# Seven products in a four-sum form, extended to the mixers' input projection, in a macaron block kernel

## What is computed

```python
def swiglu_ffn(h, w_in, w_out):                    # w_in (2048, 2*5632), w_out (5632, 2048)
    gate, up = jnp.split(h @ w_in, 2, axis=-1)
    return (jax.nn.silu(gate) * up) @ w_out

def mixer_block(h, w_in, b_in, ...):
    z = h @ w_in + b_in                            # 2048 -> 1024 pool | 2048 conv | 4096 gates
    pooled = causal_multiscale_pool(u_pool)        # windows 2, 4, 8, 16
    a  = (group_map(pooled) * pool_scale) @ pool_w_proj
    c  = causal_depthwise_conv(glu(u_conv))        # 31 taps
    bb = silu(layernorm(c)) @ conv_w_proj
    return (sigmoid(g_a) * a + sigmoid(g_b) * bb) @ w_out

x = x + 0.5 * swiglu_ffn(rmsnorm(x), ffn1...)
x = x + mixer_block(rmsnorm(x), ...)
x = x + 0.5 * swiglu_ffn(rmsnorm(x), ffn2...)
return rmsnorm(x)
```

## Time and profile before

| | before |
|---|---|
| median of 3 runs | 4974.64 us |
| profiled execution, slowest core (6) | 4988.0 us |
| other cores in it | 4966.1 to 4980.6 us |
| TensorE busy | 4608.7 us (92%), 24754 matmuls |
| VectorE busy | 3335.2 us (67%) |
| ScalarE busy | 1409.4 us (28%) |
| DMA from GpSimd's queue | 407.40 MB, 52.8% of the 16 engines' span |
| DMA from SyncE's queue | 330.97 MB, 20.7% |
| mean granted TensorE clock | 0.972 of 2.4 GHz |

### The profile page before, as it was taken

One profiled execution on the slowest core, in us unless ns is written; L12 is line 12 of the kernel. 1 busy time (PEld: TensorE's weight loads), 2 busy tenths in 40 slices (PEclk: granted clock), 3 DMA queues, 4 the chain that ended last, 5 costly groups with the idle time before them and its releaser, 6 DMA issues.

```text
span 4988.0 us, 68651 instructions; the slowest of 8 cores (4966.1 to 4988.0 us)
## 1 busy us (share of the span) xinstructions
PE 4608.7 (92%) x24754; PEld 2446.8 (49%) x24754; DVE 3335.2 (67%) x3734; ACT 1409.4 (28%) x2136; POOL 311.6 (6%) x508
## 2 busy tenths in 40 slices
PE   4999889999999997899999999999999989789996
PEld 3888668865444443344444444444444434334442
DVE  5655436768978885467778888866455656455567
ACT  2333223532213232234321112333213223222232
POOL 0000110000000000000000000000100000000000
PEclk9999999999999999999999999999999999899998
DMA  4799996777657699998757875485996585784743
GB/s 105 117 161 133 146 162 114 195 190 177 115 119 133 156 148 156 166 137 205 164 115 170 213 173 99 106 168 127 175 232 121 126 183 125 157 178 108 129 110 143
DMA packets 175227, 742.76 MB, mean 149 GB/s; under 512 B 17840, under 2 KB 18992, under 8 KB 146736
## 3 DMA queue, kind: packets, MB, share of 16 engines
q0 software_dynamic: 77056, 407.40, 52.8%
q1 hardware_dynamic: 97840, 330.97, 20.7%
HBM read 907.26 MB, written 225.57 MB: 227 GB/s over the span
## 4 chain that ended last, share of the span: by engine, by line
PE 67%; DMA 16%; DVE 10%; issue 5%; ACT 2%; another core or an unknown queue 0%; DVEq 0%; SPq 0%; ACTq 0%; POOLq 0%; POOL 0%
PE PSUM L551 66%; DMA raw<-ffn_w_in 6%; DVE BIG L469 5%; DVE BIG L472 4%; DMA outA<-BIG 3%; DMA BIG<-X2A 1%; ACT BIG L482 1%; DMA X1B<-BIG 1%; DMA BIG<-CD 1%; PE PSUM L563 1%; DMA BIG<-GD 1%; DMA BIG<-xA 1%; DMA BIG<-MD 1%; DMA BIG<-X2B 1%; DMA BIG<-X1A 1%
## 5 line engine op out<-in xcount | busy, mean ns | idle before, releaser
L551 PE MATMUL PSUM<-BIG 128*128 128x512 bf16 (+1 forms) x13200 | 2405.5, 341 | 148.9 <-ACT BIG L482 69.1
L551 PE MATMUL PSUM<-BIG,raw 128*128 128x512 bf16 (+2 forms) x11380 | 2253.7, 357 | 148.0 <-DVE BIG L469 69.0
L551 PEld LDWEIGHTS PSUM<-BIG 128*128 128x128 f16 x13200 | 1292.0, 99 | 1212.9 <-issue 220.2
L551 PEld LDWEIGHTS PSUM<-BIG,raw 128*128 128x128 f16 x11380 | 1119.3, 99 | 1231.1 <-issue 201.0
L469 DVE TENSOR_TENSOR BIG<-BIG 128x1024 f32<-128x1024 f32 (+10 forms) x934 | 703.8, 780 | 691.4 <-ACT BIG L482 637.7
L469 DVE TENSOR_TENSOR BIG<-raw 128x2048 f16<-128x2048 f16 (+3 forms) x816 | 821.7, 1014 | 448.1 <-PE PSUM L551 227.8
L482 ACT ACTIVATE PSUM<-PSUM 128x512 f32<-128x512 f32 (+1 forms) x680 | 339.5, 499 | 1498.8 <-PE PSUM L551 1491.6
L482 ACT ACTIVATE BIG<-PSUM 128x1024 f32<-128x1024 f32 (+3 forms) x684 | 469.0, 686 | 833.3 <-PE PSUM L551 785.0
L472 DVE SCALAR_TENSOR_TENSOR BIG<-BIG,CST 128x1024 f32<-128x1024 f32 (+2 forms) x520 | 638.3, 1231 | 28.6 <-DVE BIG L469 4.7
L469 DVE TENSOR_TENSOR BIG<-PSUM,BIG 128x1024 f32<-128x1024 f32 (+3 forms) x532 | 475.3, 894 | 142.5 <-PE PSUM L551 109.8
L482 ACT ACTIVATE BIG<-BIG 128x1024 f32<-128x1024 f32 (+2 forms) x388 | 338.0, 904 | 429.4 <-DVE BIG L469 333.4
(11 more groups left out here) (56 smaller groups left out, 448.3 us busy)
## 6 DMA issues: line engine op xcount, KB each, us to landing
raw<-ffn_w_in POOLq DMA_DIRECT2D x176, 1024.0 KB, 10.8
raw<-w_in POOLq DMA_DIRECT2D x112, 512.0 KB, 7.0
raw<-ffn_o SPq DMA_DIRECT2D x56, 896.0 KB, 9.0
raw<-ffn_o SPq DMA_DIRECT2D x32, 1024.0 KB, 6.9
ffn_o<-ffn_w_out POOLq DMA_DIRECT2D x32, 896.0 KB, 18.6
X2A<-BIG POOLq DMA_DIRECT2D x24, 1024.0 KB, 14.9
X1A<-BIG SPq DMA_DIRECT2D x32, 528.0 KB, 10.2
ffn_o<-ffn_w_out POOLq DMA_DIRECT2D x16, 1024.0 KB, 26.7
```

The lines of the kernel that those rows point to most:

```text
L551: ins = e.matmul(d, a, r, start=(start and i == 0), stop=(stop and i == last), skip_group_check=True)
```

## The change

- The seven products take another form: four sums of weight quarters (each one quarter long) and four sums of token quarters in place of five and five. Three bank copies and one copy to SBUF remain on ScalarE; the lower two result quarters are added out of PSUM after step 5, the upper two are read from PSUM by whoever uses them after step 6. For half A the two column groups run step by step in turn, in banks 0 to 3 and 4 to 7.
- `mix_a` uses it too: 28 units of 1 MB in place of 56 of 512 KB. All 1056 columns of A are now done for all of them. Results are multiplied by 1/rms on VectorE. The mixers' other gate goes to DRAM (GA); the pooling projection moves to `mix_b` (A) or behind it (B); MX goes through DRAM.
- FFN1 of A starts from x times its gain, without 1/rms: products of the gate are scaled before the silu, and the gate once more for the up product. Statistics are taken inside the first unit (`x_stats`). x comes in nine pieces in the order of use, and GpSimd's queue holds back all weights but the first unit until x has landed.
- `add_x` is gone: chunk 0 of FFN1 loads x and adds it on VectorE. In FFN2, chunk 1 of A and all of B load the sum, add, and store plainly; so does chunk 2 of A. Accumulating DMAs stay in chunk 1 of FFN1 and chunk 0 of FFN2 of A.
- The last chunk of FFN2 of B does its last three units in two column halves of 256, and norms and stores the first half beside the second. The background final norm of A puts load, square and norm in separate steps.

```diff
-    PRODUCTS = ((("raw", 0), 3), (("raw", 3), 2), (("d", 0), 6), (("rs", 1), 0), (("rs", 0), 1), (("es", 0), 4),
-                (("es", 1), 5))
-
-    def make_sums(ws, sm, nk, part):
+    PRODUCTS = ((("raw", 0), F11, 0), (("sum", 2), FT3, 1), (("sum", 1), FT2, 0), (("raw", 1), F21, 2),
+                (("sum", 0), FT1, 3), (("raw", 3), FT4, 0), (("sum", 3), F22, 3))
+
...
         if part == 0:
-            vt(c2(L), sm.d[:, 0:L], rq[:, 0, :], rq[:, 3, :], ALU.add, rb, [sm.b[2]])
+            vt(c2(L), s[2], q[:, 0, :], q[:, 2, :], ALU.subtract, rb, [b[2]])
         elif part == 1:
-            vt(c2(2 * L), sm.rs[:, :, 0:L], rq[:, 0::2, :], rq[:, 1::2, :], ALU.add, rb, [sm.b[0]])
+            vt(c2(L), s[0], q[:, 2, :], q[:, 3, :], ALU.add, rb, [b[0]])
+        elif part == 2:
+            vt(c2(L), s[1], s[0], q[:, 0, :], ALU.subtract, rb + [b[0]], [b[1]])
         else:
-            vt(c2(2 * L), sm.es[:, :, 0:L], rq[:, 2:0:-1, :], rq[:, 0::3, :], ALU.subtract, rb, [sm.b[1]])
...
+            vt(c2(L), s[3], q[:, 1, :], s[1], ALU.subtract, rb + [b[1]], [b[3]])
...
-                if step == 0:
-                    act(bk(V, w), bk(G, w), AF.Copy, [b_bank[G]], [b_bank[V]])
-                elif step == 1:
-                    act(t[:, 0, :], bk(U, w), AF.Copy, [b_bank[U]], [tb[0]])
-                elif step == 2:
-                    act(bk(H, w), bk(G, w), AF.Copy, [b_bank[G]], [b_bank[H]])
-                    while late:
-                        late.popleft()()
...
+        def do(step, p, wait=None):
+            base = bases[p]
+            G, Z, K, V = range(base, base + 4)
+            job = jobs[p]
+            start = step < 2
+            if first and start and (p == 0 or hook is None):
+                part(p, step, range(nk - 1, nk), False, True)
+            else:
+                part(p, step, range(nk), start, True)
+            run = (lambda fn: fn()) if wait is None else wait.append
+            if step == 0:
+                act(bk(K, w), bk(G, w), AF.Copy, [b_bank[G]], [b_bank[K]])
+            elif step == 1:
+                drain(early)
+                act(job.t7, bk(Z, w), AF.Copy, [b_bank[Z]], job.b7)
+            elif step == 2:
+                act(bk(V, w), bk(G, w), AF.Copy, [b_bank[G]], [b_bank[V]])
+            elif step == 4:
+                act(bk(Z, w), bk(V, w), AF.Copy, [b_bank[V]], [b_bank[Z]])
+            elif step == 5:
+                drain(late)
+                vt(c1(2 * w), job.low, PSUM[:, G:G + 2, 0:w], job.t7.unsqueeze(1).to_broadcast([128, 2, w]), ALU.add,
+                   [b_bank[G], b_bank[Z]] + job.b7, job.blow)
+                if job.lower is not None:
+                    if np_ == 1 or wait is not None:
+                        run(lambda: job.lower())
+                    else:
+                        lows.append(job.lower)
+                if p == np_ - 1:
+                    drain(lows)
+            elif step == 6:
+                run(lambda: job.upper(PSUM[:, K:K + 2, 0:w], [b_bank[K], b_bank[V]]))
+            if p == 0 and step == 0 and nxt is not None:
+                make_sums(ws, nk, 3, sm)
+            if p == np_ - 1 and nxt is None and step == 2:
+                drain(late)
+            elif p == np_ - 1 and nxt is not None:
+                if step == 2:
+                    drain(late)
+                    nxt(0)
                 elif step == 4:
-                    act(t[:, 1:3, :], PSUM[:, V:V + 2, 0:w], AF.Copy, [b_bank[V], b_bank[U]], tb[1:3])
-                    vt(c1(2 * w), t[:, 3::-3, :], t[:, 0, :].unsqueeze(1).to_broadcast([128, 2, w]), t[:, 2:0:-1, :],
...
+                def lower():
+                    vt(c1(2 * w), t.t[:, 2:4, :], t.t[:, 2:4, :], x.t[:, 2:4, :], ALU.add, b[2:4] + x.b[2:4], b[2:4])
+
+                def upper(ps, pb):
+                    if x is None:
+                        act(t.t[:, 0:2, :], ps, AF.Copy, pb, b[0:2])
+                    else:
+                        vt(c1(2 * w), t.t[:, 0:2, :], ps, x.t[:, 0:2, :], ALU.add, pb + x.b[0:2], b[0:2])
+                    if homes is None:
+                        put(m, p, t)
+                    if xts and p == np_ - 1 and m + len(xts) < 8 and (not full or len(xts) == 1):
+                        load_x(m + len(xts))
+                    if full:
+                        work = [lambda a=a: square(p, a, m, t, x) for a in range(2)]
+                        if un is not None:
+                            work += [lambda: gain(p, m, t)]
+                        if m < 7:
+                            late4.extend(work)
+                        else:
...
+            def early_norm():
+                stats(0, cut)
+                for j in range(8):
+                    for a in range(2):
+                        bg.append(lambda j=j, a=a: norm(j, a, 0, cut))
+
+            for m in range(5, 8):
+                u.again(n0 + m - 5, Cols(self.hid, cut, w), [job(m, cut, w)], early_norm if m == 5 else None)
+            drain(late)
+            drain(late4)
+            stats(cut, w)
+            flush(bg)
+            for m in range(8):
+                for a in range(2):
+                    norm(m, a, cut, w)
 
...
+        def pair(fin_upper, fin_lower=None, both=None):
+            def job(p):
+                t = head.popleft() if head else rot("t", tiles)
+                r = t.rows()
+
+                def lower():
+                    scale2(t.t[:, 2:4, :], t.b[2:4], t.t[:, 2:4, :], t.b[2:4], S, p, w)
+                    if fin_lower is not None:
+                        early.append(lambda: fin_lower(p, r[:, 1, :], t.b[2:4]))
+
+                def upper(ps, pb):
+                    scale2(t.t[:, 0:2, :], t.b[0:2], ps, pb, S, p, w)
+                    early.append(lambda: fin_upper(p, r[:, 0, :], t.b[0:2]))
+                    if both is not None:
+                        early.append(lambda: both(p, r, t.b))
+
+                return Job(t.t, t.b, lower, upper)
+
+            return [job(p) for p in range(np_)]
...
+
+        def step1b(k):
             if k >= 1 and k <= NKD:
                 square(k - 1)
             idle(7.0)
 
         def step2(k):
-            if k >= 2:
-                norm(k - 2)
             if k < NKD:
                 load(k)
-            idle(7.0)
+            idle(8.0)
+
+        def step2b(k):
+            if k >= 1 and k <= NKD:
+                norm(k - 1)
+            idle(8.0)
 
         for k in range(NKD + 2):
...
+    PIECES = ((0, 4), (8, 12), (4, 8), (12, 16))
+    xp = [(p, lo, hi) for p in range(2) for lo, hi in PIECES]
+    xp[7:] = [(1, 12, 15), (1, 15, 16)]
+    for i, (p, lo, hi) in enumerate(xp):
+        dma(view(x0_at[p][lo], (hi - lo, 528), F32), dr["xA"][:, lo:hi, p * 528:(p + 1) * 528], [], b_X0[p][lo:hi],
+            s_x0[i])
+    W.gate = b_X0[1]
+    F = Ffn("ffn1", HA, HFA, HIA, "x", "X1", un=True)
...
+    def x_stats(p):
+        if p == 0:
+            x_sums(0, 3)
+            x_done(0)
+            for i in range(4):
+                x_prep(1, i)
+                if i < 2:
+                    x_sums(1, i)
+        else:
+            ts = [t for i in (2, 3) for _, t in x_tiles(i)]
+            for t in ts[1:]:
+                vt(c1(528), ts[0].t, ts[0].t, t.t, ALU.add, [ts[0].b, t.b], [ts[0].b])
+            x_sum(1, ts[0], False, True)
+            x_done(1)
...
-    shared["w_in"] = plain(inp["w_in"], D, INW, 128)
+    mp = [(16 + j, 8 + j) for j in range(8)]
+    for lo, n in ((0, 4), (24, 8), (40, 8)):
+        mp += [(lo + 2 * i, lo + 2 * i + 1) for i in range(n)]
+    shared["w_in"] = quads(np.asarray(inp["w_in"], np.float32).reshape(D, INW), half, mp)
```

1214 lines of the change are left out of this document (689 added, 525 removed).

## The result

The changed kernel takes **4836.85 us**, the median of 4 runs, against 4975.37 us for the kernel before on the same chip: a ratio of **0.971** (95% interval 0.9685 to 0.9735). A later repetition of the same pair (run e14) gave 0.9701 (0.9687 to 0.9716). Runs in which one die shows a lower granted clock and a longer span (5141 us here) are left out of every ratio. The kernel is faster, as forecast, but 4643 us and the range of 4560 to 4800 were missed: less than half of the gain of 332 us came.

A forecast was written before the change was run, and what follows sets the result against it. TensorE was taken as the bound: 4453 us of full-rate matmuls plus 535 lost. Afterwards 4366 plus 290 lost give 4656, less 13 for the runs' median: 4643 us, range 4560 to 4800.

The forecast's parts named there:

- The products of the mixers, 87 us: Mixers: fewer or cheaper matmuls save 39 us in A and 48 in B, all on the path.
- rival 4: Mixers: each unit's first product waits for VectorE's results or 1 MB weights, the 87 us fall to nothing; 4730 us, chance 0.04.
- The start, 54 us: Kernel start: x lands sooner, second unit starts near 56 us, 50 us lost instead of 104; bounds 30 and 65.
- `add_x`, 109 us: FFN1, chunk 1: without accumulating transfers, lost time falls from 84 to 30 in A, 87 to 32 in B; bounds 30, 135.
- Rival 1: FFN1 and FFN2: DMA engines stay as crowded and the waits stay; 4825 us, halfway 4730, chance 0.15.
- FFN2 of B, 60: FFN2 of B: load and use in separate steps leave 36 of 96 us lost; bounds 20 and 80.
- FFN2 of A, 19: FFN2 of A: lost time falls from 64 to 45 us; bounds -10 and 35.
- The tail, 9: Kernel end: last norms 512 columns wide, tail 36 us instead of 45; bounds 0 and 20.
- +2 and +4 us of lost time: Mixers: cost of VectorE's added sums and passes, covered by 105 us of slack between B's last norm row's store and read.
- Rival 2: Mixers: VectorE has too much work; if taps cannot move, 100 us return as waits; 4743 us, chance 0.12.
- FFN1 of B, 32: FFN1 of B: 32 of 87 us stay lost, part of the 109 us gained in FFN1.
- Rival 3: Every unit: three waits for ScalarE's bank copies make it slower from 1.0 us per unit; 5135 at 0.5 each, chance 0.03.

The follow-up runs named there:

- e14: The changed kernel itself once more, nothing altered, repeated against the kernel before; 0.9701 of the kernel before.
- e13: Changed kernel with all background work barred while either mix_a runs and made up right behind each mixer; 5052 us, one execution.
- e4: Changed kernel with the squares of the first x written in 16 bits and all summed by TensorE as 16-bit matmuls; 0.9657 of the kernel before.
- e7: Kernel before without its accumulating transfers of x in FFN1's chunk 1, first residual left out of the result; 0.986 of the kernel before.
- e8: Kernel before with only the changed kernel's background final norm of A, load and use in separate steps; profiled span 4928 us against 4988.
- e1: Changed kernel with background convolution taps barred while either mix_a runs and run afterwards; 0.9838 of the kernel before.
- e3: Changed kernel with both mixers' deferred sigmoids and biased copies behind the next unit's last bank copy; B's mix_a lost 42 us instead of 65.
- e6: Changed kernel with B's deferred sigmoids behind the next unit's last bank copy, and Silu made of Sigmoid, Identity and a product; 0.9652 of the kernel before.
- e5: Changed kernel with longer load-to-use distances: 24 us before a channel's first tap, 14 and 7 for half B's x; 0.9693 of the kernel before.
- e9: Changed kernel with three of half B's form pairs started one group earlier, load-to-use distances left as they were; 0.9777 of the kernel before.
- e10: Changed kernel with three form pairs started earlier and distances of 24 us before first taps, 10 and 5 for half B's x; 0.9688 of the kernel before.
- e12: Changed kernel with 16-bit squares, B's sigmoids behind copies, earlier form pairs, longer load-to-use distances, 20 us before re-read convolution rows; 0.9653 of the kernel before.
- e2: Changed kernel with Sigmoid in place of Silu on half A's convolution rows, a product left out; B's mix_a lost 48.5 us instead of 65.

## Why the prediction was wrong, point by point

- **The products of the mixers, 87 us: right as work, nothing as time.** The matmuls of 352 columns are gone, and the prices hold: windows of 100 us at a granted clock of 1.00 have 890 weight loads of the 264-column products (400 to 500 us) and 464 of the 512-column ones (1400 to 1500 us). But the 93 us more of lost time ate the 87, so rival 4's outcome, nothing for the products, came in these stages. Its mechanism, a wait at each unit's first product, did not: e13 shows one long first unit and four waits behind the group products. No run has the rest of the change with the mixers in the old form.
- **The start, 54 us: 38 came**, inside the bounds. The step that was mis-sized is the second unit "near 56 us": it started at 78. I left out the 100 sums in 32 bits, 29 us of TensorE; e4 shows 10 us of them on the path, the rest is not tried.
- **`add_x`, 109 us: 73 came.** The cause is shown by e7, in the chunk where I put it. FFN1 of A hit 30. What I mis-sized is B: 30 us stayed in its chunk 1 in e7 too, so my 87 to 32 took for one cause what were two. Rival 1, that the waits stay, is refuted for the stores and w_in units: TensorE has no direct wait for a w_in unit left in FFN1 of A (10.3 us before) and one of 3.6 us behind an X1A store (17.4 before). It came in a small part by the w_out units: the two waits over 5 us that are left (6.7 us at 251, 6.3 at 531) stand behind VectorE, which stood 11.5 and 11.7 us for such a unit. The page of the Trainium skill that I cited (DMA: Bandwidth & Descriptors, Issuing engines are not separate DMA queues) says that a change of the issuing engine saves only the time to issue. e7 does not speak against that, since it takes the bytes away and not the queue.
- **FFN2 of B, 60: 47 came,** and e8 shows the mechanism by itself at 55. At first SyncE issues a load 4 to 9 us behind a store of outA instead of 17 us. It still stands for outA later on, 83 us in 11 waits with one of 15.3 (core 0; 157 us in 14 before), so my sign "not standing 10 us or more" failed; the compute engines no longer wait behind it. **FFN2 of A, 19: nothing came** (63 as before). A bound of -10 covered it; no run takes it apart.
- **What I overlooked are the w_out units.** They come by SyncE's in-order queue, which now also loads the sums. TensorE waited for them 33.3 us in 7 waits (core 0), the longest 8.0 us in FFN1 of B, 9.7 in FFN2 of A and 11.1 in FFN2 of B; before, it was 6.1 us in one. VectorE stood 161 us in 32 waits for them, before 25 us in 5. No run tests what puts them late.
- **The tail, 9: 14 came.** 24 norms of 512 columns took 15.99 us where the 16 of 1024 took 19.22; the split is worth a little more than I said.
- **VectorE and the mixers: the step that failed.** I wrote "I cost it at +2 and +4 us of lost time, and name the cover: that slack". It was +38 in A and +55 in B with A's `mix_b`. VectorE was not fuller than before (342 of 428 us in A and 325 of 406 in B, 80% each, where it was 83 and 81%), and not over 90% as I had it. Rival 2, which asks for the sum of its work, is refuted by e1 in A: with VectorE at 66% the mixer lost more. I had compared amounts of work, and the queues' order decided. Of what the mixers lose now, 22 us in B are sigmoids and silus ahead of the copies (e3, e6), 15 more in B and 21 in A are background work ahead of its loads and between the passes (e13; e5, e9 and e10 show the loads), and 42 in A and 28 in B are foreground, A's costed as if the first unit could be covered like any other (e13). In the old form a block product of the mixers needed no sums of its weights, no bank copy and no result of the unit before; that this is why the same VectorE load lost 26 us there is argued, not tried.
- **FFN1 of B, 32: 51.** By chunks it is 19, 10 and 24 (before 10, 55 and 9), so chunk 1 did what I said and more, and the others lost 24 more. In chunk 2 (core 7) VectorE stands 11.1 us for a CD row of half A's convolution and TensorE 6.9 us behind it; e12 made that distance 20 us and gained nothing clear of noise. The rest is open. (The chunks have 7, 7 and 8 pairs of hidden-channel blocks; e12's expectation counts its 20 and 5 us as if the first had 8.)
- **Rival 3** (three bank copies a unit) had a price of 1.0 us per unit. FFN1 of A has 136 runs of seven steps and loses 30 us for all causes, so the copies alone cost next to nothing. They cost only where something stands ahead of them.
- **The range** was also added up wrongly. The low ends are 30 + 30 + 20 - 10 + 0 beside the products' 87, and with 6 us for the mixers they give 4824 us, not 4800; the high ends give 4559, not 4570. 4837 lies above either. For the mixers' lost time, the one term with no row for it, I gave no bound at all.
- **The signs:** "wrong if the lost time stays above 400 us" came, with 444. "No wait over 5 us for weights or X1 stores in chunk 1" holds for TensorE's direct waits, but not for the 6.3 us behind VectorE and its w_out unit.

SyncE's queue in FFN2 of B of the changed kernel, the answer to the earlier trace rows:

```profile
4319.51 0.34 SPq L503 DMA_DIRECT2D outA<-BIG  x1
4328.29 0.32 SPq L503 DMA_DIRECT2D BIG<-X2A  x1
4337.12 0.34 SPq L503 DMA_DIRECT2D outA<-BIG  x1
4340.74 0.32 SPq L503 DMA_DIRECT2D BIG<-X2A  x1
```

and VectorE at the end, the answer to the earlier trace rows:

```profile
4815.46 15.99 DVE L490 SCALAR_TENSOR_TENSOR BIG<-BIG,CST,RSB 128x512 f32<-128x512 f32 x24
```

What stays open: the foreground of A's `mix_a` (only its place is shown, not tried apart), FFN2 of A, what the change is worth without the mixers' part, and why the cores differ more than before (44 us from the first to the last, 22 before).

## What to carry to other kernels

Read a stage's length before and after beside its work: the mixers had 87 us less to do and took no less time. When a change makes TensorE need another engine more often, do not cost it by that engine's free time: list what can stand in its in-order queue at that moment and what each of these waits for. A background operation is put behind its load by landing time, not by a model's idle time, and a distance that is enough in a quiet stage is not in one where the queue runs ahead; make the whole schedule move with it, or the wait is only moved to the stage's end. In ScalarE's queue, work whose result is needed a unit later goes behind the copies that TensorE needs now.

## What the runs showed of the hardware that I had not expected

- **A wait costs a quarter to six tenths as much again in clock.** On core 0, 56.5 us of waits came with 71 us lost in A's `mix_a`, 48 with 69 in B's, and 27 with 43 in A's of e13. The granted clock of A's stretch is 0.95, between the two levels of 1.2 and 2.4 GHz, and 16 matmuls right behind a wait of 8 us took 3.4 to 3.7 us instead of 1.96. Without background work B's mixer has 1.00 and e1's A mixer, with the longest waits, 0.92.
- **DRAM-to-DRAM accumulating transfers held other DMAs up, in both queues.** Eight transfers of about 1 MB a half cost 45 and 29 us of TensorE's time (e7). While they ran, w_out units from SyncE's queue took 19.7 us to land and without them 7.0. Whether accumulating or going from DRAM to DRAM makes them so, no run tells.
- **A function table change is 1283 ns, and two of them go with every silu between sigmoids:** 16 loads, 20.5 us of ScalarE in B's mixer, 1 with Sigmoid alone (e2).
